# Requests for the weights of the fifth and sixth expert, placed behind the first two row gathers of a mixture-of-experts stage

## The reference, cut to what matters

```
a   = rows @ w_gate[e]                  # 1024 x 256
u   = rows @ w_up[e]                    # 1024 x 256
y_e = (silu(a) * u) @ w_down[e]         # 256 x 1024
out[row] = sum over its two experts of weight * y_e[row]
```

## Time and profile before

| what | value |
|---|---|
| median of 3 runs | 1856.75 us (1853.15 to 1857.49) |
| the profiled execution, its own time | 1854.39 us |
| its span | 1852.7 us |
| mean granted clock of PE | 0.895 |
| PE busy | 1494.2 us (81%) |
| DVE busy | 718.8 us (39%) |
| ACT busy | 573.3 us (31%) |
| POOL busy | 344.5 us (19%) |
| moved by the DMA engines | 322.11 MB, 174 GB/s over the span |

### The profile page before, as it was taken

How to read it: one execution, slowest core, us unless ns; L and a number is a source line. 1 busy time by engine, 2 the same in 40 slices (tenths; PEclk the granted TensorE clock), 3 DMA queues, 4 the chain that set the end, 5 groups by cost and what they waited for, 6 DMA issues and landing times.

```text
span 1852.7 us, 31456 instructions
## 1 busy us (share of the span) xinstructions
PE 1494.2 (81%) x11216; PEld 1147.1 (62%) x11216; DVE 718.8 (39%) x1738; ACT 573.3 (31%) x1008; POOL 344.5 (19%) x235
## 2 busy tenths in 40 slices
PE   2999876979978489988459998679799883999782
PEld 2768876966856455555247698669668563555451
DVE  5137988034351411111331389870444324111114
ACT  4334543255512111111143355333554110111112
POOL 3311241210300022222014013313003000222210
PEclk9998986989998699999769899779899985999996
DMA  4211240112431799999631121302023327999994
GB/s 170 91 46 47 96 135 14 58 56 66 136 127 36 302 338 387 390 392 394 228 126 46 46 92 59 127 20 75 35 70 132 125 104 292 356 380 391 399 393 179
DMA packets 92012, 322.11 MB, mean 174 GB/s; under 512 B 15376, under 2 KB 15760, under 8 KB 75232
## 3 DMA queue, kind: packets, MB, share of 16 engines
q1 hardware_dynamic: 74800, 287.36, 41.7%
q0 software_dynamic: 10240, 17.33, 2.8%
q10 hardware_dynamic: 6832, 15.61, 2.3%
HBM read 302.49 MB, written 34.01 MB: 182 GB/s over the span
## 4 chain that ended last, share of the span: by engine, by line
PE 39%; issue 26%; SPq 13%; DVE 9%; DMA 6%; POOL 4%; ACT 2%; DVEq 0%; ACTq 0%; POOLq 0%
PE ps L719 12%; SPq L547 8%; PE ps L696 7%; PE ps L985 6%; SPq L553 4%; POOL gate_up_low L1993 3%; PE ps L706 3%; PE ps L1006 3%; DMA gu_ring<-w_expert_up 3%; PE ps L909 2%; PE ps L974 2%; PE ps L884 1%; PE ps L902 1%; DVE pr L1262 1%; DMA expert<-yrow 1%
## 5 line engine op out<-in xcount | busy, mean ns | idle before, releaser
L719 PE MATMUL ps<-x_high,chunk_high_a 128*128 128x264 f32 x896 | 266.6, 298 | 16.9 <-POOL gate_up_low L1993 11.7
L719 PE MATMUL ps<-x_high,gate_up_low 128*128 128x264 f32 (+1 forms) x928 | 272.9, 294 | 0.0
L719 PE MATMUL ps<-x_low,chunk_high_a 128*128 128x264 f32 x896 | 262.5, 293 | 0.0
L1993 POOL TENSOR_TENSOR gate_up_low<-gu_ring,chunk_high_a 128x1024 fp32r<-128x1024 f32 x56 | 135.3, 2428 | 467.8 <-ACT chunk_high_a L1678 467.8
L719 PEld LDWEIGHTS ps<-x_high,chunk_high_a 128*128 128x128 f32 x896 | 177.4, 198 | 21.5 <-issue 21.0
L719 PEld LDWEIGHTS ps<-x_high,gate_up_low 128*128 128x128 f32 (+1 forms) x928 | 181.7, 196 | 0.6
L719 PEld LDWEIGHTS ps<-x_low,chunk_high_a 128*128 128x128 f32 x896 | 177.6, 198 | 0.0
L1580 DVE COPY r<-ps 128x512 f32<-128x512 f32 x64 | 44.3, 692 | 316.7 <-PE ps L974 316.7
L696 PE MATMUL ps<-gate_up_low,x_high 128*128 128x512 f32 (+1 forms) x400 | 165.3, 413 | 0.0
L2044 POOL DMA_INDIRECT r<-xrow,idx x64 | 61.4, 959 | 537.8 <-issue 296.4
L1916 ACT ACTIVATE r<-ps 128x256 f32<-128x256 f32 x64 | 24.6, 384 | 316.7 <-PE ps L985 316.7
(11 more groups left out here) (317 smaller groups left out, 2960.2 us busy)
## 6 DMA issues: line engine op xcount, KB each, us to landing
gu_ring<-w_in SPq DMA_DIRECT2D x20, 2048.0 KB, 9.2
gu_ring<-w_expert_gate SPq DMA_DIRECT2D x22, 1024.0 KB
gu_ring<-w_expert_up SPq DMA_DIRECT2D x22, 1024.0 KB
dn_ring<-w_expert_down SPq DMA_DIRECT2D x44, 512.0 KB
r<-w_expert_down SPq DMA_DIRECT2D x40, 512.0 KB
expert<-w_expert_gate SPq DMA_DIRECT2D x12, 1024.0 KB
expert<-w_expert_up SPq DMA_DIRECT2D x12, 1024.0 KB
expert<-w_expert_down SPq DMA_DIRECT2D x24, 512.0 KB
```

The lines of the kernel that those rows point to most:

```text
L719: last = mm(o[:, lo:hi], w[:, c, quarter(name, j)], x[:, c, lo:hi], start=c == 0 and k == 0, stop=c == KC - 1 and k == 2)
L1993: G.tensor_tensor(low[:, :, cols], w[:, :, cols], high[:, :, cols].bitcast(F32), ALU.subtract).then_inc(sem["low_p"], 1)
```

## The change

One wait of SP is replaced by two. Before, SP requested the gate and up matrices of expert 4 when the last router product was done. Now it first waits until gather 0 (`xg0`) and gather 1 (`xg1`) have landed:

```diff
                 for b in range(2):
                     load_gate_up(HEAD + b, b)
                     load_down(HEAD + b, b)
-                sp.wait_ge(*at("pe_done", LAST["ro"] + 1))
-                settle(sp)
+                for u in range(2):
+                    sp.wait_ge(*at(f"xg{u}", 16))
+                    settle(sp)
                 load_gate_up(HEAD + 2, 2)
                 sp.wait_ge(*at("base_ready", 1))
                 settle(sp)
```

## The result

| | before | changed |
|---|---|---|
| median of 5 runs | 1856.75 us | 1864.94 us |
| lowest to highest | 1853.15 to 1862.19 | 1862.16 to 1868.05 |
| ratio of the runs | | 1.0044, 95% interval 1.0023 to 1.0065 |
| profiled execution, span | 1852.7 us | 1866.4 us |

The account below looks back on a forecast made before the run. The weight stream through the DMA engines was taken to bound the expert stages. Its later flow, 5.0 us in layer 0 plus 4.5 in layer 1, added 9.5 to 1856.75: 1866.3 us, own range 1863 to 1871, whole range 1859 to 1874.

Parts of the forecast that it names:

- The stream bounds the stage, PE does not: Expert stages: the weight stream's end sets the stage's end; PE gives away 21.5 us per layer waiting for weights.
- The gather at 3.5 us: Gather 1, ending SP's new waits, lands 3.5 us after its start (bounds 1.9 and 7.95); SP reacts in 0.15.
- The block and its rate: Weights requested behind the new waits: 6.29 MB at 425 GB/s, 14.8 us, with gathers 2 and 3 16.2 us.
- 0.7 us for each gather in the block: Gathers moving among the block's weights: 0.12 MB each, adding 0.7 us of flow apiece.
- Expert 4's absence from the idle time as a cost: Expert 4's gate and up, 2.10 MB, leave the routing's idle time and cost 4.9 us of flow later.
- the second hole: Idle stretch of the DMA engines before expert 6's weights flow, 655.8 to 661.0 us in layer 0; the change closes it.
- PE's waits: PE's waits for weights grow from 21.5 to nearer 31 us per layer, beginning some five experts earlier.
- The rival of the late gathers: First gathers take 7.95 us by themselves, so SP starts 4.45 us later per layer: 18.4 us slower, 1875; chance 0.07.
- The rival of slack in the stream: Later weight stream: a deeper backlog wins back 4 us per layer, leaving 1.5 us, 1858; chance 0.11.
- The ring gives 5 experts of outstanding requests: Weight requests late in the stage: 5 experts outstanding when PE is the waiting one, so the stream isn't starved.

Follow-up runs that it names:

- e1: Changed kernel, but expert 4's gate and up requested early as before, gather waits only ahead of expert 5; 1859.21 us beside 1859.04 for before.
- e3: The changed kernel, with PE also waiting for expert 4's gate and up before its first transposes; ratio to before 1.0047.
- e2: The kernel before, without gather waits, expert 4's gate and up requested behind expert 5 and expert 4's down; 1860.93 us beside 1859.04.
- g1: The kernel before, without gather waits, expert 4's gate and up requested directly in front of expert 5's; 1860.29 us beside 1858.97.
- e4: The changed kernel, with SP also waiting for expert 0's gate-up result to be copied out before requesting expert 4; 1880.94 us beside 1859.04 for before.
- f2: f1 with waits for gathers 0 and 1 in front of the last 2.1 MB (expert 5's up, expert 4's down); 1847.32 us, ratio to before 0.9951.
- f1: The kernel before, with 2.1 MB of expert 5 (gate, down) requested in the routing's idle time, a small routing table moved; 1858.22 us beside 1858.26.

## Why the prediction was right

The direction, the place and the size were right: 9.5 us forecast, 8.2 measured and 8.0 in the stages, 1864.94 us inside the range. The steps one by one:

- *The stream bounds the stage, PE does not.* Shown by e1 and e3 from both sides: PE 4 us sooner or 9 us later changes nothing beyond 1 us.
- *The gather at 3.5 us.* Gather 1, which ends the waits, takes 2.9 us, and SP follows after 0.24 us instead of 0.15: 3.1 us together instead of 3.65. Expert 4's request came 37.3 us after expert 2's in layer 0 instead of the forecast 37.9, and 37.1 instead of 38.5 in layer 1, where gather 1 itself also began 0.8 us earlier. Together 1.9 us too much in the sum, and 9.5 - 1.9 = 7.6 is near the measured 8.0. The gather, 1.1 us of this, is the mis-sized term. The other 0.8 us is the chance in the gathers' start told above; without it the stages would have shown some 8.8 us.
- *The block and its rate.* No row shows where the block ends, since no hole follows, as forecast. The table of four kernels above bears the reckoning out to half a us per step in layer 0, and to 1 us in layer 1. The prediction charged 0.7 us for each gather in the block; no run isolates this term.
- *Expert 4's absence from the idle time as a cost.* Right only together with its other half: e2 moves the same 2.1 MB and costs next to nothing, since the second hole takes them. In the changed kernel they cost because the waits had already used that hole up.
- *PE's waits.* Forecast some 31 us per layer, measured 25.5. The waits begin four experts sooner, not five. PE had 9.6 us more slack in layer 0 (4.9 sooner, 4.7 longer) and 8.8 in layer 1 (5.5 and 3.3), 18.4 in all. Of these only 7.9 went into waits. The gate-ups took 9.9 us more: over their five groups 256.1 us beside 246.2. Three groups of the changed kernel:

```profile
L986 PE MATMUL ps<-expert,r 128*64 128x256 f32 x384 | 51.8, 430 | 9.8 <-DMA expert<-w_expert_up 7.8 <-DVE r L1581 1.9
L986 PE MATMUL ps<-r 128*64 128x256 f32 x320 | 43.4, 432 | 11.1 <-DMA r<-w_expert_up 11.1
L986 PE MATMUL ps<-pr,r 128*64 128x256 f32 x320 | 40.0, 406 | 11.0 <-DMA pr<-w_expert_up 10.8
```

Their means were 402, 382 and 382 ns before. Ten gate-ups of the changed kernel's two stages, and five of before's, took 5.0 to 5.4 us instead of 3.67, each after a wait of 1.8 to 2.8 us for weights. One is shown here, with the three us in the middle of it, in which the granted clock is 0.50, the lower of its two levels.

```profile
815.22 5.36 PE L986 MATMUL ps<-r 128*64 128x256 f32 x32 [2.02 <-DMA r<-w_expert_up]
```

```profile
816.50:819.50 3.00, 3.00 (x18) 2.10 (x16) 0.00 (x0) 0.00 (x0) 0.00 (x0) 0.50 1.00 330
```

Not every such wait is followed by this: at 851.17 a gate-up takes 3.67 us after a wait of 2.36. That slowdown is off the path that sets the end, and it was left out of the working.

- *The rival of the late gathers.* It fell: the gather is quick on empty engines. But I read its 8 us as a gather queued with 4 MB of weights, and e2 and g1 showed otherwise: neither 6.3 MB around it nor 4.2 MB requested ahead of it make it later. The Trainium skill (DMA: Bandwidth & Descriptors, on queues and arbitration) lets each DMA engine take turns between queues. g1 agrees with that in so far as the gather doesn't wait for all that was requested before it. But it still loses 5 us, and the rate drops only 5 us after its start, so turns alone don't account for the loss; its cause stays open. The prediction did not hang on the reason, only on 3 to 4 us for a gather without weights.
- *The rival of slack in the stream.* A backlog won next to nothing back: in e4 7.4 us more of hole cost 6.7 us in layer 0 and 7.4 in layer 1.
- *"The ring gives 5 experts of outstanding requests."* It doesn't get that far. The last up matrix of before's layer 0 is on the chain with 27.2 us from request to landing:

```profile
867.35 27.18 DMA gu_ring<-w_expert_up
```

At 382 GB/s that is 10.4 MB, the weights of 3.3 experts. What was concluded from it holds all the same, since the engines are full to the end.

## What to carry to other kernels

Where one resource is the bound to the end of a stage, count its idle holes before that: in these runs a start of PE, or a late request, was worth only the hole that it opened or closed, to about 1 us per layer. A request moved out of an idle stretch is free while another hole is left for it, and costs its full flow once the same edit closes that hole. Letting the small urgent transfer go first does pay, if the large ones are moved ahead of it into the idle time, and not behind it: the same two waits cost 8 us in the changed kernel, and f2, which has them, is 9 us faster than f1, which has not.

## What the runs showed of the hardware that was not expected

- An indirect gather of about 0.12 MB takes 2.9 to 3.2 us on empty engines, 4.2 us beside 1.05 MB of weights, 7.3 us beside 2.1 MB, and then hardly more: 8.0 us beside 6.3 MB, whichever of them are requested first. Beside 4.2 MB and more the total rate drops only 5 us after its start.
- Weights alone flow at 422 to 425 GB/s (stretches of 8 and 13 us), the long stream with gathers and scatters among them at 382 to 387 GB/s (stretches of 101 to 246 us). Short stretches with a gather in them lie lower: 366 GB/s over 12 us in e2.
- After waits of 1.8 to 2.8 us some gate-ups run in part at TensorE's lower clock level (granted clock 0.50), and take up to 5.4 us instead of 3.67. More waits make more of them: ten in the changed kernel, five before.
